# The partial sums of squares of eight RMS norms: added on VectorE, summed over partitions twice a norm

## The chip, the cores and the metric

One core of a Trainium2 chip runs the whole network of the reference in one launch. The metric is the device time of one execution in microseconds (us); what is compared are medians over several executions.

## The reference, cut to what matters

The input is one sequence of 256 tokens ("latents", 1024 features) with 256 context tokens beside it, all float32. The work is two blocks of two layers; a layer of the first block is a gated feed-forward network (ffn), a token mixer (mix) and a second ffn, a layer of the second is an attention mixer (even, odd) and a mixture of experts (peer). What matters here is that an RMS norm stands between every two of these parts:

```python
def rmsnorm(x, w):
    x32 = x.astype(jnp.float32)
    r = lax.rsqrt(jnp.mean(x32 * x32, axis=-1, keepdims=True) + EPS)
    return (x32 * r).astype(x.dtype) * w
...
    xl = xl + 0.5 * g1l * swiglu(modulate(rmsnorm(xl, norm_w[0]), sh1l, sc1l), w_ffn1_in, w_ffn1_out)
    ...
    hl = modulate(rmsnorm(xl, norm_w[1]), sh2l, sc2l)
    ...
    xl = xl + g2l * mix_l
    xl = xl + 0.5 * g3l * swiglu(modulate(rmsnorm(xl, norm_w[2]), sh3l, sc3l), w_ffn2_in, w_ffn2_out)
```

So for each token the squares of its 1024 features are summed, and the root's inverse scales the token.

## The kernel before

**Layout.** `x` and `h` are held as 128 partitions x KC = 8 chunks x tokens: feature 128 k + p of a token lies on partition p of chunk k. A stage works on T = 512 tokens (latents and context) or on TL = 256 (latents alone, where the context is no longer needed). A sum over a token's features is thus a sum over 8 chunks and then over 128 partitions.

**Split products.** Weights and activations are each split into a rounded high part and a low rest, and `split_product` (L1030 to L1034) makes three matmuls of them: high x high, high x low, low x high. ScalarE (ACT) rounds, VectorE (DVE) or GpSimd (POOL) subtracts to get the low part. A matmul has a 128x128 stationary operand (PEld loads it) and 512 or 256 moving columns.

**Stages.** They run one after the other, in this order: mods, norm1_0, ffn1_0, norm2_0, mix_0, norm3_0, ffn2_0, norm1_1, ffn1_1, norm2_1, mix_1, norm3_1, ffn2_1, final1, even_norm, even, peer_norm_0, peer_0, odd_norm, odd, peer_norm_1, peer_1, final2. Every engine has one queue of instructions, written in program order, and semaphores order the engines among each other. Weights come through a ring of 8 slots that SyncE (SP) fills; a slot is loaded again when `panel_done` (or, for modulation weights, `mod_units_read`) says that it has been read.

**The end of a stage, where the change lies.** An ffn ends with 8 output panels, one for each chunk dc of x. A panel is 22 chunks of the hidden layer x 3 matmuls = 66 matmuls (`ffn_stage` of the tensor block, L1129 to L1146); its weights come in two halves, each rounded by ACT (`round_out`, L1580) once the panel half that used the buffer before is through, and then split by DVE (`split_out`, L2054). The mixers (mix, even, odd) end with 8 panels of 8 x 3 = 24 matmuls (`out_product`, L1148 to L1177) with `round_proj` (L1637) and `split_proj` (L2114) for weights. There the first two panels are made up to their last input chunks before the last part of the attention is there, so panels 0 and 1 end close together. mix_0 and even have 2 buffers for rounded weights, so that panel 2's weights are rounded only once panel 0 is through; mix_1 and odd have 4.

After each panel `add_to_x` (L2043) adds it to chunk dc of x (`x_added`), `square` (L1527) on ACT squares the chunk into a scratch tile, and `sums` (L1088 to L1096) on TensorE multiplies the squares, as the stationary operand, by a column of ones: one output column for each 128 tokens, accumulated over the 8 chunks in one bank. One such product in float32 comes out as two pairs of weight load and matmul, so a chunk costs 8 pairs with 512 tokens and 4 with 256. The sums of chunk dc - 1 stand in TensorE's queue behind panel dc (`sums_behind`), so those of chunks 0 to 5 stand between panels, and those of 6 and 7 behind the last panel. After an ffn there is one scratch tile (the last chunk of `h`), after a mixer there are two (in `work`). Then `norm_stage` takes over: ACT rounds the next stage's first weight unit (L1515), then takes the root (L1549), DVE the reciprocal (L2017), TensorE spreads it over the partitions (L1078), and DVE scales x (L2022).

In three of the four ffns (ffn1_0, ffn2_0, ffn1_1) DVE also makes products for the modulation in between (`mod_sums`, L1948 and L1950): up to two weight units, 8 operations, in an output panel.

Norms that don't follow an ffn or mixer: norm1_0 (behind mods), even_norm (behind final1), odd_norm and final2 (behind peer).

## Time and profile before

| | |
|---|---|
| median of 3 runs | 4516.12 us (4515.93, 4516.12, 4524.71) |
| profiled execution | 4522.2 us, its span 4520.4 us |
| mean granted TensorE clock in it | 0.973 of full speed |
| TensorE busy | 4294.9 us, 95% of the span |
| VectorE busy | 3221.8 us, 71% |
| ScalarE busy | 1825.0 us, 40% |
| GpSimd busy | 1423.2 us, 31% |

The span is the time from the first to the last instruction of the profiled execution; 1.8 us of its own time lie around it. In the rows below a time is in us from the span's start, "x8" is a run of eight instructions shown as one row, and a bracket gives the idle time of the engine ahead of the row and what ended it.

### The profile page before, as it was taken

To read this page: it belongs to the slowest core of one execution; us is meant where nothing else is said; L and a number is where in the kernel's file an instruction comes from. 1 tells how busy PE (TensorE), PEld (TensorE's weight loads), DVE (VectorE), ACT (ScalarE), POOL (GpSimd) and SP (SyncE) were. 2 spreads that over 40 slices of the span, in tenths; PEclk is the share of its full clock that TensorE was granted. 3 is DMA by queue.
4 is the path that set the end of the run, shared out by engine and by line. 5 is a ranking of instruction groups with operands and counts; after the bars stand their busy time and mean duration, and the time that the engine had idled before them with its cause. 6 is when DMAs were issued, how large, how long until landed. Compare 5 with 4: busy or idle time off the path is not lost.

```text
span 4520.4 us, 62059 instructions
## 1 busy us (share of the span) xinstructions
PE 4294.9 (95%) x24455; PEld 3842.2 (85%) x24455; DVE 3221.8 (71%) x5137; ACT 1825.0 (40%) x2986; POOL 1423.2 (31%) x701
## 2 busy tenths in 40 slices
PE   7999899999999998999999899799999999999999
PEld 5887678887888798767899899799998799999887
DVE  5764547876887575464589899498886757785776
ACT  3233242233233434254233577233334544444444
POOL 0000300000000100000277688667772028665443
PEclk9999999999999998998999999899999999999999
DMA  6543214544544264201467799899995146678884
GB/s 269 221 158 124 75 38 177 223 177 184 226 184 183 93 246 169 79 34 47 133 218 236 244 331 330 289 373 351 359 352 181 39 166 220 211 243 275 288 288 163
DMA packets 286689, 926.50 MB, mean 205 GB/s; under 512 B 19136, under 2 KB 170816, under 8 KB 212288
## 3 DMA queue, kind: packets, MB, share of 16 engines
q1 hardware_dynamic: 249536, 788.30, 49.1%
q0 software_dynamic: 36864, 134.23, 8.4%
q8 instruction: 195, 3.19, 0.3%
q14 instruction: 94, 0.77, 0.1%
HBM read 837.52 MB, written 84.93 MB: 204 GB/s over the span
## 4 chain that ended last, share of the span: by engine, by line
PE 77%; DVE 12%; DMA 5%; ACT 3%; POOL 2%; issue 1%; SPq 0%; DVEq 0%; ACTq 0%; POOLq 0%
PE bank L1032 22%; PE bank L1034 21%; PE bank L1033 21%; DVE work L2356 3%; PE bank L1203 2%; PE bank L1397 2%; DMA gates<-work 2%; PE bank L1018 2%; PE bank L1187 2%; PE bank L1022 1%; PE bank L1094 1%; DMA work<-in_up_rows,work 1%; DVE work L2463 1%; POOL weight_ring_low L2611 1%; PE bank L1194 1%
## 5 line engine op out<-in xcount | busy, mean ns | idle before, releaser
L2611 POOL TENSOR_TENSOR weight_ring_low<-weight_ring,up_high 128x1024 fp32r<-128x1024 f32 x240 | 650.2, 2719 | 1138.4 <-ACT up_high L1761 1136.4
L1034 PE MATMUL bank<-peer_h_high,weight_ring_low 128*128 128x256 f32 (+2 forms) x2240 | 702.7, 314 | 0.0
L1032 PE MATMUL bank<-peer_h_high,up_high 128*128 128x384 f32 (+1 forms) x2048 | 648.5, 317 | 35.6 <-POOL weight_ring_low L2611 33.7
L1033 PE MATMUL bank<-h_low,up_high 128*128 128x384 f32 (+1 forms) x2048 | 638.2, 312 | 0.0
L1032 PE MATMUL bank<-h_high,in_high 128*128 128x512 f32 (+1 forms) x1280 | 465.3, 364 | 5.6 <-DVE weight_ring_low L2002 5.2
L1848 ACT ACTIVATE down_high<-weight_ring 128x1024 fp32r<-128x1024 f32 x256 | 257.4, 1054 | 517.0 <-PE bank L1034 511.5
L1034 PE MATMUL bank<-h_high,weight_ring_low 128*128 128x512 f32 (+1 forms) x1280 | 464.7, 363 | 0.0
L1033 PE MATMUL bank<-h_low,in_high 128*128 128x512 f32 (+1 forms) x1280 | 464.6, 363 | 0.0
L2578 POOL TENSOR_SCALAR h<-work,params 128x256 f32<-128x256 f32 x12 | 10.9, 921 | 1439.8 <-DVE work L2266 1439.8
L1034 PEld LDWEIGHTS bank<-peer_h_high,weight_ring_low 128*128 128x128 f32 x2240 | 429.8, 192 | 3.8
L1032 PEld LDWEIGHTS bank<-peer_h_high,up_high 128*128 128x128 f32 x2048 | 394.3, 193 | 40.6 <-POOL weight_ring_low L2611 38.3
L2620 POOL TENSOR_TENSOR weight_ring_low<-weight_ring,down_high 128x1024 fp32r<-128x1024 f32 x128 | 314.8, 2459 | 321.3 <-ACT down_high L1848 321.2
L2383 DVE TENSOR_TENSOR weight_ring_low<-weight_ring,down_high 128x1024 fp32r<-128x1024 f32 x128 | 307.1, 2399 | 150.1 <-ACT down_high L1848 150.1
L1033 PEld LDWEIGHTS bank<-h_low,up_high 128*128 128x128 f32 x2048 | 394.0, 192 | 0.0
L1032 PE MATMUL bank<-hidden_high,down_high 128*128 128x384 f32 x1016 | 339.5, 334 | 0.5 <-DVE hidden_low L2383 0.5
L1034 PE MATMUL bank<-hidden_high,weight_ring_low 128*128 128x384 f32 x1016 | 339.4, 334 | 0.0
L1033 PE MATMUL bank<-hidden_low,down_high 128*128 128x384 f32 x1016 | 339.4, 334 | 0.0
L1767 ACT ACTIVATE work<-bank 128x384 f32<-128x384 f32 (+1 forms) x256 | 112.3, 439 | 496.2 <-PE bank L1034 492.0
L1515 ACT ACTIVATE in_high<-weight_ring 128x2048 fp32r<-128x2048 f32 x88 | 168.7, 1917 | 330.3 <-PE bank L1034 310.8
L1032 PEld LDWEIGHTS bank<-h_high,in_high 128*128 128x128 f32 x1280 | 242.3, 189 | 45.2 <-issue 7.8
L1033 PEld LDWEIGHTS bank<-h_low,in_high 128*128 128x128 f32 x1280 | 242.3, 189 | 37.4
L1034 PEld LDWEIGHTS bank<-h_high,weight_ring_low 128*128 128x128 f32 x1280 | 242.2, 189 | 37.3
(364 smaller groups left out, 10527.3 us busy)
## 6 DMA issues: line engine op xcount, KB each, us to landing
weight_ring<-in_up SPq DMA_DIRECT2D x128, 1024.0 KB, 5.6
weight_ring<-in_down SPq DMA_DIRECT2D x128, 1024.0 KB, 6.6
weight_ring<-in_mod_w SPq DMA_DIRECT2D x112, 1024.0 KB, 5.4
weight_ring<-in_ffn_in SPq DMA_DIRECT2D x88, 1024.0 KB, 6.8
weight_ring<-in_ffn_out SPq DMA_DIRECT2D x64, 704.0 KB, 4.4
gates<-work SPq DMA_DIRECT2D x40, 1024.0 KB
gelu<-work SPq DMA_DIRECT2D x64, 384.0 KB
work<-gates SPq DMA_DIRECT2D x16, 1536.0 KB
```

The costliest lines, as they stand in the source:

```text
L1018: mm(ps[bank][:, 0:cols], w_high[:, k, w(j0 + kc)], high[:, kc, 0:cols], start=kc == 0, stop=False)
L1032: mm(dst, w_high, a_high, start=first, stop=False)
L1033: mm(dst, w_high, a_low, start=False, stop=False)
L1034: return mm(dst, w_low, a_high, start=False, stop=last)
L1187: mm(ps[m % 4][:, 0:j["nk"]], j["q"][q], j["k"], start=True, stop=True).then_inc(scores_done, 1)
L1515: A(high_of(name)[1][:, k % 2, :], ring[:, u % SLOTS, :], ACT.Copy).then_inc(in_rounded, 1)
L1767: A(gelu_out[:, n // 2 % 2, n % 2, 0:t], ps[UP_BANKS[n % 3]][:, 0:t], ACT.Gelu).then_inc(gelu_ready, 1)
L1848: A(down_high[:, m % 2, k, :], ring[:, u % SLOTS, k * D:k * D + D], ACT.Copy).then_inc(down_rounded, 1)
L2356: V.scalar_tensor_tensor(row, row, 1.0, picked_h, ALU.mult, ALU.mult, accum_out=picked_acts[:, q:q + 1])\
L2383: return V.tensor_tensor(dst, src, high.bitcast(F32), ALU.subtract)
L2611: G.tensor_tensor(ring_low[:, slot, w], ring[:, slot, w], up_high[:, n % 3, :].bitcast(F32), ALU.subtract)\
L2620: G.tensor_tensor(ring_low[:, slot, D:], ring[:, slot, D:], down_highs[l][:, m % 2, 1, :].bitcast(F32), ALU.subtract)\
```

## The change

For the eight norms that follow an ffn or a mixer (norm2_0, norm3_0, norm1_1, norm2_1, norm3_1, final1, peer_norm_0, peer_norm_1; `joined`), the squares of chunks 1 to 6 are no longer summed over partitions one by one. Chunk 0's squares lie in a tile that serves as the total; `join_squares` on DVE adds the squares of chunks 1 to 6 to it, each ahead of DVE's wait for panel k + 1. TensorE then sums over partitions twice: once the total of chunks 0 to 6, and once chunk 7, which ACT writes into the same tile after the first of the two is through. Both stand behind the last panel (`joined_sums`). Chunks 1 to 6 have two scratch tiles of their own: banks 4 and 5 of PSUM behind an ffn, two tiles of `work` behind a mixer. A square waits for the join that frees its tile. The other norms keep their way; the counts of `summed` are kept by stage.

```diff
@@ -424,7 +424,7 @@
         ones_ready, lam_sums, lam_exps = sem("ones_ready"), sem("lam_sums"), sem("lam_exps")
         params_loaded, x_loaded, ctx2_loaded = sem("params_loaded"), sem("x_loaded"), sem("ctx2_loaded")
         tables_loaded, gains_ready = sem("tables_loaded"), sem("gains_ready")
-        squares_made = sem("squares_made")
+        squares_made, squares_added = sem("squares_made"), sem("squares_added")
         slot_full = [sem(f"slot_full{s}") for s in range(SLOTS)]
         panel_done = sem("panel_done")
         passed = {e: sem(f"{e}_passed") for e in ("pe", "act", "dve", "pool")}
@@ -500,12 +500,12 @@
                 before = stages[i - 1][0]
                 s["order"] = (2, 3, 4, 5, 7, 6, 0, 1) if name == "odd_norm" else tuple(range(KC))
                 s["sum_bank"], s["scale_bank"] = (7, 4) if name == "final2" else (2, 5) if before == "peer" else (5, 4) if before == "final" else (7, 6)
-                s["before"] = before
+                s["before"], s["joined"] = before, before in ("ffn", "mix", "even", "odd")
                 if kind == "norm":
                     s["next"] = stages[i + 1][1:]
                 norm_of[stages[i - 1][1]] = name, s
         counts = dict(norm=0, added=0, ffn=0, free=4, square=0, root=0, lora=0, conv=0, tile=0, out=0, mod=0,
-                      peer=0, ptile=0, rtile=0, parts=0, scaled=0, normed=0, rounds=0, keys=0)
+                      peer=0, ptile=0, rtile=0, parts=0, scaled=0, normed=0, rounds=0, keys=0, summed=0, joined=0)
 
 
         take = scratch()
@@ -731,7 +731,11 @@
 
             if s["before"] in ("mods", "final"):
                 return h[:, k, :]
-            return h[:, KC - 1, :] if s["before"] == "ffn" else work[:, k % 2 * T:k % 2 * T + T]
+            if not s["joined"]:
+                return work[:, k % 2 * T:k % 2 * T + T]
+            if k in (0, KC - 1):
+                return h[:, KC - 1, :] if s["before"] == "ffn" else work[:, 0:T]
+            return ps[4 + k % 2][:, :] if s["before"] == "ffn" else work[:, (1 + k % 2) * T:(2 + k % 2) * T]
 
         def job(q, k, nk, v, scale, prep=None):
             return dict(q=q, k=k, nk=nk, v=v, scale=scale, prep=prep)
@@ -827,6 +831,8 @@
             if kind in ("norm", "final"):
                 counts["norm"] += 1
                 counts["square"] += KC
+                counts["summed"] += 2 if s["joined"] else KC
+                counts["joined"] += (KC - 2) * s["joined"]
                 counts["root"] += 1
                 counts["scaled"] += KC
             if kind == "norm":
@@ -1100,6 +1106,23 @@
                 if name in norm_of and 0 <= k < KC:
                     sums(*norm_of[name], k)
 
+            def joined_sums(name):
+
+
+                if name not in norm_of:
+                    return
+                name, s = norm_of[name]
+                q, t = at[name]["square"], s.get("t", TL)
+                for last in (False, True):
+                    if last:
+                        pe.wait_ge(squares_ready, q + KC)
+                    else:
+                        pe.wait_ge(squares_added, at[name]["joined"] + KC - 2)
+                    for tt in range(t // P):
+                        i = mm(ps[s["sum_bank"]][:, tt:tt + 1], squares_of(name, s, 0)[:, tt * P:tt * P + P], ones[:, 0:1],
+                               start=not last and tt == 0, stop=last, skip_group_check=True)
+                    i.then_inc(summed, 1)
+
             def norm_stage(name, s):
                 if s["before"] == "mods":
                     return
@@ -1142,8 +1165,7 @@
                             o = split_product(ps[dc % 4][:, 0:t], out_part(2 * dc + half)[:, w], ring_low[:, u % SLOTS, w],
                                               ffn_high(kc)[:, 0:t], ffn_low[:, kc, 0:t], kc == first_chunks[0], kc == second_chunks[-1])
                         o.then_inc(panel_done if half else out_half, 1)
-                    sums_behind(name, dc - 1)
-                sums_behind(name, KC - 1)
+                joined_sums(name)
 
             def out_product(name, t):
 
@@ -1172,9 +1194,7 @@
                     if dc >= OUT_BANKS:
                         pe.wait_ge(x_added, at[name]["added"] + dc - OUT_BANKS + 1)
                     product(dc, range(KC - late, KC) if dc < 2 else range(KC)).then_inc(panel_done, 1)
-                    if dc:
-                        sums_behind(name, dc - 1)
-                sums_behind(name, KC - 1)
+                joined_sums(name)
 
             def attention(name, beside_first_scores=lambda: None):
                 jobs, dsts, subs = job_lists[name]
@@ -1516,14 +1536,18 @@
 
             def square(name, s, k):
 
-                t, kc, buffers = s.get("t", TL), s["order"][k], 1 if s["before"] == "ffn" else 2
+                t, kc = s.get("t", TL), s["order"][k]
                 if s["before"] == "final":
                     act.wait_ge(scaled_ready, at[name]["scaled"] - KC + k + 1)
                     act.wait_ge(ctx2_loaded, 16)
                 else:
                     act.wait_ge(x_added, at[name]["added"] - KC + k + 1)
-                    if k >= buffers:
-                        act.wait_ge(summed, KC * at[name]["norm"] + k - buffers + 1)
+                    if not s["joined"] and k >= 2:
+                        act.wait_ge(summed, at[name]["summed"] + k - 1)
+                    if s["joined"] and k == KC - 1:
+                        act.wait_ge(summed, at[name]["summed"] + 1)
+                    elif s["joined"] and k >= 3:
+                        act.wait_ge(squares_added, at[name]["joined"] + k - 2)
                 A(squares_of(name, s, k)[:, 0:t], x[:, kc, 0:t], ACT.Square).then_inc(squares_ready, 1)
 
             def square_behind(name, k):
@@ -1545,7 +1569,7 @@
                 if "next" in s:
                     round_unit(*s["next"], 0)
                 if s["before"] != "mods":
-                    act.wait_ge(summed, KC * (at[name]["norm"] + 1))
+                    act.wait_ge(summed, at[name]["summed"] + (2 if s["joined"] else KC))
                     A(square_sum[:, tiles], ps[s["sum_bank"]][:, tiles], ACT.Sqrt, bias=eps[:, 0:1], scale=1.0 / D).then_inc(root_ready, 1)
                 if "next" in s:
                     round_unit(*s["next"], 1)
@@ -2044,6 +2068,16 @@
                                                ALU.mult, ALU.add)
                 return i
 
+            def join_squares(name, k):
+
+
+                if name in norm_of and 1 <= k < KC - 1:
+                    name, s = norm_of[name]
+                    t, total = s.get("t", TL), squares_of(name, s, 0)
+                    dve.wait_ge(squares_ready, at[name]["square"] + k + 1)
+                    wait_for(dve, squares_added, at[name]["joined"] + k - 1)
+                    V.tensor_tensor(total[:, 0:t], total[:, 0:t], squares_of(name, s, k)[:, 0:t], ALU.add).then_inc(squares_added, 1)
+
             def ffn_stage(name, s):
                 t, f0, p0 = s["t"], at[name]["ffn"] * FC, plan.panel0[name]
                 o0 = at[name]["ffn"] * KC
@@ -2088,6 +2122,7 @@
                 for dc in range(KC):
                     if dc + 1 < KC:
                         split_out(2 * dc + 2)
+                    join_squares(name, dc - 1)
                     dve.wait_ge(panel_done, p0 + 2 * FC + dc + 1)
                     add_to_x(dc % 4, s["gate"], dc, t).then_inc(x_added, 1)
                     if dc + 1 < KC:
@@ -2117,6 +2152,7 @@
             def add_outs(name, gate, t):
 
                 for dc in range(KC):
+                    join_squares(name, dc - 1)
                     dve.wait_ge(panel_done, proj_panel(name) + dc + 1)
                     add_to_x(dc % OUT_BANKS, gate, dc, t).then_inc(x_added, 1)
                     if dc + proj_buffers(name) < KC:
```

## Rows read from the trace of the kernel before

**Rows 1.** The profile page: span, busy time of TensorE, and the chain that ended last.
```profile
span 4520.4 us, 62059 instructions
...
PE 4294.9 (95%) x24455; PEld 3842.2 (85%) x24455; DVE 3221.8 (71%) x5137; ACT 1825.0 (40%) x2986; POOL 1423.2 (31%) x701
...
PE 77%; DVE 12%; DMA 5%; ACT 3%; POOL 2%; issue 1%; SPq 0%; DVEq 0%; ACTq 0%; POOLq 0%
```

**Rows 2.** Groups by line and shape, PE: the norms' sums (count, busy, mean; idle before).
```profile
L1094 PE MATMUL bank<-ones,work 128*128 128x1 f32 x288 | 41.3, 265 | 9.2 <-ACT work L1527 9.1
L1094 PE MATMUL bank<-ones,h 128*128 128x1 f32 x288 | 40.1, 262 | 4.6 <-ACT h L1527 4.6
```

**Rows 3.** Timeline of PE (start, duration), a seam of ffn1_0's output panels and the next sums.
```profile
312.23 0.39 PE L1034 MATMUL bank<-ffn_high_last,weight_ring_low 128*128 128x512 f32 x1
312.46 0.95 PE L1094 MATMUL bank<-ones,h 128*128 128x1 f32 x8
313.27 0.49 PE L1032 MATMUL bank<-ffn_high,out_high 128*128 128x512 f32 x1
...
328.37 0.94 PE L1094 MATMUL bank<-ones,h 128*128 128x1 f32 x8
```

**Rows 4.** Timeline of PE in ffn1_0's input panels, first and last of 55 rows.
```profile
199.68 0.39 PE L1034 MATMUL bank<-h_high,weight_ring_low 128*128 128x512 f32 x1
...
211.92 0.39 PE L1034 MATMUL bank<-h_high,weight_ring_low 128*128 128x512 f32 x1
```

**Rows 5.** Timeline of PE around mix_1's first two seams (256 columns).
```profile
1541.54 0.28 PE L1034 MATMUL bank<-parts_mix,weight_ring_low 128*128 128x256 f32 x1
1542.97 0.60 PE L1094 MATMUL bank<-ones,work 128*128 128x1 f32 x4 [1.16 <-ACT work L1527]
1543.44 0.36 PE L1032 MATMUL bank<-parts_mix,proj_more 128*128 128x256 f32 x1
...
1543.76 0.28 PE L1034 MATMUL bank<-parts_mix,weight_ring_low 128*128 128x256 f32 x1
...
1546.28 0.28 PE L1034 MATMUL bank<-parts_mix,weight_ring_low 128*128 128x256 f32 x1
...
1546.76 0.36 PE L1032 MATMUL bank<-parts_mix,proj_more 128*128 128x256 f32 x1
```

**Rows 6.** Timeline of PE and DVE around mix_0's first seam (512 columns).
```profile
620.28 0.39 PE L1034 MATMUL bank<-parts_mix,weight_ring_low 128*128 128x512 f32 x1
621.72 1.05 PE L1094 MATMUL bank<-ones,work 128*128 128x1 f32 x8 [1.05 <-ACT work L1527]
622.63 0.47 PE L1032 MATMUL bank<-parts_mix,proj_wide 128*128 128x512 f32 x1
...
621.17 1.23 DVE L2114 TENSOR_TENSOR weight_ring_low<-weight_ring,proj_wide 128x1024 fp32r<-128x1024 f32 x1 [0.27 <-ACT proj_wide L1637]
```

**Rows 7.** Groups by line and shape, DVE: an add-sized operation that reads a bank.
```profile
L2022 DVE TENSOR_TENSOR h<-x,bank 128x512 f32<-128x512 f32 x56 | 37.6, 682 | 13.2 <-PE bank L1078 13.2
...
L2022 DVE TENSOR_TENSOR h<-x,bank 128x256 f32<-128x256 f32 x16 | 6.5, 416 | 2.0 <-PE bank L1078 2.0
```

**Rows 8.** Timeline of DVE in ffn1_1's fullest output panel: last split, next residual add.
```profile
1377.26 1.62 DVE L2054 TENSOR_TENSOR weight_ring_low<-weight_ring,out_high 128x1408 fp32r<-128x1408 f32 x1
1381.00 0.88 DVE L2043 SCALAR_TENSOR_TENSOR x<-bank,gate,x 128x256 f32<-128x256 f32 x2 [2.11 <-PE bank L1034]
```

**Rows 9.** Timeline of DVE in ffn2_1's output panels, two residual adds one panel apart.
```profile
1738.32 0.48 DVE L2043 SCALAR_TENSOR_TENSOR x<-bank,gate,x 128x256 f32<-128x256 f32 x1 [0.86 <-PE bank L1034]
...
1746.68 0.48 DVE L2043 SCALAR_TENSOR_TENSOR x<-bank,gate,x 128x256 f32<-128x256 f32 x1 [0.86 <-PE bank L1034]
```

**Rows 10.** Timeline of PE, DVE and ACT at the end of mix_0.
```profile
660.16 0.95 PE L1094 MATMUL bank<-ones,work 128*128 128x1 f32 x8
...
660.36 0.88 DVE L2043 SCALAR_TENSOR_TENSOR x<-bank,gate,x 128x256 f32<-128x256 f32 x2 [5.52 <-PE bank L1034]
...
661.27 0.63 ACT L1527 ACTIVATE work<-x 128x512 f32<-128x512 f32 x1 [5.76 <-DVE x L2043]
662.30 1.91 ACT L1515 ACTIVATE in_high<-weight_ring 128x2048 fp32r<-128x2048 f32 x1 [0.39 <-issue]
```

**Rows 11.** A matmul of peer_1 after idle time, and busy time by stretch with PEclk.
```profile
3890.22 0.39 PE L1032 MATMUL bank<-peer_h_high,up_high 128*128 128x256 f32 x1 [1.94 <-DVE weight_ring_low L2383]
...
3891.00:3895.00 4.00, 4.00 (x23) 4.00 (x22) 3.96 (x3) 0.10 (x1) 1.41 (x1) 0.57 0.00 0
```

## The prediction

> **What bounds the kernel now.** I read the page first. TensorE is busy 4294.9 us of a span of 4520.4 us, and the chain that ended last runs through it for 77% [rows 1]. So an operation taken off TensorE is worth its time, if nothing else holds the same place. The page is only a mean, so I went to the groups by line for what the change touches: the norms' sums are 576 pairs of weight load and matmul, some 263 ns each if one believes the mean, 81 us busy together [rows 2]. That overstates them, since a matmul's duration holds its flight through the array and neighbours overlap. What counts is by how much a group of sums pushes the next matmul back, and that only the timeline tells.
>
> At a seam between two of ffn1_0's output panels, the last matmul of a panel starts at 312.23 and the first of the next at 313.27, 1.04 us later, with the 8 pairs of one chunk between them [rows 3]. Where no sums are, the 55 rows from 199.68 to 211.92 give 54 steps of 0.2267 us, and they go over a panel's end without a break [rows 4]. So 8 pairs push back by 1.04 - 0.23 = 0.81 us. The period tells a little more: 328.37 - 312.46 = 15.91 us from sums to sums, against 66 x 0.2267 = 14.96 us for the matmuls alone, so 0.95 us go with each seam; the 0.14 us beyond the gap are slow first steps of the next panel (its first matmul takes 0.49 where 0.39 is usual) [rows 3]. With 256 columns the plain step is (1546.28 - 1543.76) / 21 = 0.12 us (third to last of a panel's 24), the gap over 4 pairs 0.48, so 0.36 us of pushing back, and the two first steps take 0.32 where 0.24 is usual: 0.44 us a seam [rows 5]. In ffn2_1 the period says the same: 1746.68 - 1738.32 = 8.36 against 66 x 0.12 = 7.92 us [rows 9].
>
> **The change part by part.**
>
> *Sums taken off the seams.* In each of the eight norms the sums of chunks 0 to 5 go, those of chunks 6 and 7 are kept in number and place (as the total and chunk 7). Five norms work on 512 tokens, three on 256, so 6 x (5 x 8 + 3 x 4) = 312 pairs go. In the ffns all six seams are plain. ffn1_0, ffn2_0, ffn1_1: 3 x 6 x 0.95 = 17.1 us. ffn2_1: 6 x 0.44 = 2.6 us.
>
> *The first seam of a mixer* isn't plain: panels 0 and 1 end close together, and the sums of chunk 0 wait for its square. In mix_1 that is 1.16 us idle, and the whole seam takes 1543.44 - 1541.54 = 1.90 us [rows 5]. Panel 2 has its weights already (4 buffers), so the seam shrinks to one step: 1.78 us, with the slow steps 1.86. In mix_0 the seam takes 622.63 - 620.28 = 2.35 us, but what is late next is the split of panel 2's weights, which ends at 621.17 + 1.23 = 622.40 [rows 6]. So only 0.2 us are won there, since the 8 pairs lay in the shadow of that split. odd is built as mix_1 in this respect and even as mix_0. Five plain seams follow in each: mix_0 and even 2 x (0.2 + 5 x 0.95) = 9.9 us, mix_1 and odd 2 x (1.86 + 5 x 0.44) = 8.1 us.
>
> *The joins on DVE.* 48 adds come in. The nearest row is an operation of the same shape that reads a bank and `x`: 0.68 us with 512 columns, 0.42 with 256 [rows 7], so 30 x 0.68 + 18 x 0.42 = 28 us more on DVE. I cost them at nothing; this is the cover. In ffn1_1's panels with two modulation units, the fullest, DVE ends the split of the next panel's weights at 1378.88 and idles 2.11 us until the add at 1381.00 [rows 8]. DVE's work there hangs on the panel's start, so the shorter panel takes 0.95 of that and the join 0.68; 0.48 us stay, and the split itself, which TensorE needs, stands ahead of the join. In ffn2_1 the split hangs on the panel's half, so only the join is taken from 0.86 us [rows 9], and 0.44 stay. A mixer's panel holds add, split and join: 0.88 + 1.23 + 0.68 = 2.8 us of 24 x 0.2267 = 5.4, or 0.48 + 1.23 + 0.42 = 2.1 of 2.9. The square that a join waits for stands in ACT's queue behind the rounding for a later panel; in the ffns that is done half a panel before. In mix_1 the join of chunk 1 holds the add of panel 2 back by about 1.4 us (square and split of the early panels come late); behind it are the split for panel 6 and the add itself, and TensorE asks for that split only four panels later. If the cover were gone, each 0.1 us that all 48 joins pushed TensorE back would cost 4.8 us.
>
> *New waits.* A square of chunks 3 to 6 waits for a join, which is done about a panel before. SP's loads move with `panel_done`, nothing else of its queue changes, and POOL's queue isn't touched.
>
> *The end of a stage.* Chunk 7's square now waits also for the first of the two sums behind a mixer (behind an ffn it did already). In mix_0 those 8 pairs run from 660.16 to 661.11, the add it waits for anyway from 660.36 to 661.24, and the square starts at 661.27 [rows 10]. So the new wait ends 0.13 us before the old one: nothing, or at worst some 0.3 us for each of four mixers. The root stands behind a 1.91 us rounding as before [rows 10]. The first sums need the joins of chunks 1 to 6; in ffn1_1 I count the last one 2 us before the panel's end.
>
> *Sum.* 17.1 + 2.6 + 9.9 + 8.1 = 37.7 us. **Bounds**: if the slow first steps stay (they could belong to the seam and not to the sums), a seam is worth 0.81 or 0.36 us: 14.6 + 2.2 + 8.5 + 7.2 = 32.5 us. I take the higher one, because the plain rows go over panel ends without such steps [rows 4]. On the other side I see no more than 42 us, if late adds and half-speed steps elsewhere fall better.
>
> The Trainium skill ("TensorE: Matmul & The Clock Gate", section "LDWEIGHTS (loading the stationary operand)") prices a weight load by its columns alone, 128 / 1.2 = 107 ns, however few columns are multiplied. By it, as an estimate, the 296 pairs that don't lie in the shadow of a split would bring 31.6 us, and with the waits at the mixers' first seams 34.3 us; the seams of this trace give 0.95 / 8 = 0.119 us a pair with the slow steps and 0.101 without them, so it stands between my two sums.
>
> **The rivals.**
>
> *A, the slow steps stay:* 32.5 us less, that is 4484 us. For it: such steps also follow a seam where TensorE only waited. Against it: rows 4. 14%.
>
> *B, the ffn panels are held by the weights' chain and not by TensorE:* rounding, then split, each half a panel. Then the four ffns bring nothing: 9.9 + 8.1 = 18 us less, 4498 us. Against it: the idle time of DVE in rows 8 and 9 stands behind the split, not ahead of it. 6%.
>
> *C, the clock.* In peer_1 a matmul came 1.94 us idle, and in the stretch from 3891 to 3895 the granted clock was 0.57, mostly the lower level of 1.2 GHz [rows 11]: 23 matmuls where 4.00 / 0.12 = 33 fit. In mix_0's first seam the sums stood in the middle of such a gap; now TensorE idles from about 620.7 to 622.4 at a stretch. One fall cost 10 steps of 0.12 us there, 1.2 us; I put 1.5 us for one at mix_0, and even's gap is shorter. At most 3 us of the 37.7 for both. Part of the forecast's own spread; chance of a fall one in four. The Trainium skill (the same page, section "A second HAM failure mode: psum-queue depth-cycling") warns that short idle times between groups of matmuls make the clock swing; by that the removal could cost rather than gain at these two seams.
>
> *D, slower.* The joins stand in DVE's queue ahead of the adds. If the squares come late, the join holds add and splits, these hold the next panel, and that its square. It decides where a panel loses more than it wins: 0.48 us of cover and 0.95 won in ffn1_1, so a join would have to hold DVE 1.4 us beyond its own 0.68. At 1.5 us lost for each of the 48 joins the kernel would take 72 - 37.7 = 34 us more, 4550 us. Against it: the idle rows 8 and 9, and ACT's small share of 40% [rows 1]. 2%.
>
> *E, the change brings nothing*, because what is won before a norm is waited away behind it, on weights that come no sooner. DMA has 5% of the chain [rows 1], and the ring is loaded as slots come free, so its times move too. 3%, 4516 us.
>
> **How the numbers follow.** The forecast has 75%. The profiled execution took 4522.2 us (span 4520.4), 6 us above the median of 4516.1; a share of 37.7 / 4522.2 = 0.83% on the median is again 37.7 us, and less a quarter of a clock fall the time is 4479 us. Its own range is 4474 to 4483. A reaches to 4484, and runs of one kernel differ by some us (4515.93 to 4524.71), so the range is 4474 to 4488 us; B, D and E, 11%, are left out. This kernel can be told from no change at about 0.2%, 9 us: faster 0.95 (forecast, A, B), same 0.03 (E), slower 0.02 (D).
>
> **What would show it.** The group of the sums should have 264 pairs where 576 were. Between ffn output panels the step over a seam should be 0.23 us and the period 14.96 us (7.92 in ffn2_1); mix_1's first seam should close, mix_0's should end at the split. 48 new adds of 0.68 and 0.42 us stand on DVE ahead of the residual adds, with idle time still behind them. From the last panel to the root nothing should move. I am wrong if TensorE shows new idle time on L2054 or L2114 at the seams, if the first matmuls of a panel still take longer, if chunk 7's square waits for TensorE, or if the granted clock is lower in these stretches.

## The result, and the profile after

The changed kernel took 4480.14 us, the median of four runs (4474.47 to 4481.91), beside 4519.01 us for the kernel before: a ratio of 0.9915, with an interval from 0.9903 to 0.9928. (The kernel before has a fourth run here, of 4521.89 us, beside the three shown above.) The prediction was 4479 us, 0.9918 of the median shown, in a range of 4474 to 4488. The profiled execution took 4481.78 us, its span is 40.4 us shorter than that of before.

The page after, to be held against [rows 1]:

```profile
span 4480.0 us, 61516 instructions
...
PE 4258.5 (95%) x24143; PEld 3809.4 (85%) x24143; DVE 3228.8 (72%) x5185; ACT 1823.7 (41%) x2986; POOL 1429.5 (32%) x701
...
PE 78%; DVE 11%; DMA 5%; ACT 3%; POOL 2%; issue 1%; SPq 0%; DVEq 0%; ACTq 0%; POOLq 0%
```

TensorE has 24455 - 24143 = 312 instructions fewer and VectorE 48 more, as counted. TensorE's busy time fell by 36.4 us, its share of the chain didn't. The VectorE total went up by only 7.0 us, though the joins' own records come to 28 us. Records of neighbouring instructions overlap in part, and other groups moved too (the sum of all VectorE durations rose by 22.6 us), so a difference of busy totals doesn't price an edit.

The joins and the sums that are left, by line and form (count, duration as min/median/max, first and last start; then who waited for the line):

```profile
L2079 DVE TENSOR_TENSOR h<-h,bank x24: 414/682/689, 323.4 to 1747.5; 128x512 f32<-128x512 f32 x18, 128x256 f32<-128x256 f32 x6
L2079 DVE TENSOR_TENSOR work<-work x24: 419/555/693, 617.5 to 3600.7; 128x512 f32<-128x512 f32 x12, 128x256 f32<-128x256 f32 x12
```

```profile
L1122 PE MATMUL bank<-ones,h x56: 164/250/271, 402.5 to 1753.8; 128*128 128x1 f32 x56
...
L1122 PE MATMUL bank<-ones,work x48: 164/250/271, 648.6 to 3603.9; 128*128 128x1 f32 x48
```

With the 160 pairs of even_norm, odd_norm and final2, which the change leaves alone, these are 264, and the trace names no instruction that waited for a join.

A seam is the place in TensorE's queue between two output panels, and the period is the time from one such place to the next. TensorE's timeline in ffn1_0, over the seam that [rows 3] showed, and one panel on:

```profile
312.52 0.39 PE L1040 MATMUL bank<-ffn_high_last,weight_ring_low 128*128 128x512 f32 x1
312.75 0.39 PE L1038 MATMUL bank<-ffn_high,out_high 128*128 128x512 f32 x1
312.98 0.39 PE L1039 MATMUL bank<-ffn_low,out_high 128*128 128x512 f32 x1
...
327.48 0.39 PE L1040 MATMUL bank<-ffn_high_last,weight_ring_low 128*128 128x512 f32 x1
```

The step over the seam is 0.23 us where it was 1.04, the first matmuls of the panel take 0.39 like all others, and the period is 327.48 - 312.52 = 14.96 us where it was 15.91. So the slow steps went with the sums. In mix_1 the first seam [rows 5] is closed:

```profile
1518.25 0.28 PE L1040 MATMUL bank<-parts_mix,weight_ring_low 128*128 128x256 f32 x1
1518.37 0.28 PE L1038 MATMUL bank<-parts_mix,proj_wide 128*128 128x256 f32 x1
```

In mix_0 the first seam [rows 6] ends at the split. TensorE, and below it DVE:

```profile
613.58 0.39 PE L1040 MATMUL bank<-parts_mix,weight_ring_low 128*128 128x512 f32 x1
615.75 0.50 PE L1038 MATMUL bank<-parts_mix,proj_wide 128*128 128x512 f32 x1 [1.79 <-DVE weight_ring_low L2149]
...
614.47 1.23 DVE L2149 TENSOR_TENSOR weight_ring_low<-weight_ring,proj_wide 128x1024 fp32r<-128x1024 f32 x1 [0.27 <-ACT proj_wide L1661]
```

The split ends at 615.70 and the matmul starts at 615.75; the seam takes 2.17 us where it took 2.35, and after 1.79 us idle the steps are 0.35, 0.24 and then 0.23 us. The granted clock from 613 to 625 was 1.00, so it didn't fall.

What the change was worth, stage by stage. The stretch is that from the first matmul of a stage's output product to the start of its last one, in us, from TensorE's timeline. The second column is a second profile of the kernel before (experiment e5, below), which shows what a stretch does by itself. Further on, the mark of a norm is the start of the first matmul that spreads its scale over the partitions (L1078 before, L1084 after).

| stage | before | before again | after | after - before | predicted |
|---|---|---|---|---|---|
| ffn1_0 | 125.53 | 125.52 | 119.80 | -5.73 | -5.7 |
| mix_0 | 51.76 | 51.79 | 47.00 | -4.76 | -4.95 |
| ffn2_0 | 125.31 | 125.33 | 119.59 | -5.72 | -5.7 |
| ffn1_1 | 125.32 | 125.30 | 119.59 | -5.73 | -5.7 |
| mix_1 | 27.05 | 27.05 | 22.98 | -4.07 | -4.06 |
| ffn2_1 | 74.39 | 75.51 | 72.93 | -1.46 | -2.64 |
| even | 50.70 | 51.55 | 45.93 | -4.77 | -4.95 |
| odd | 27.05 | 27.04 | 22.99 | -4.06 | -4.06 |
| sum | | | | -36.3 | -37.7 |

One term is off, ffn2_1, and the second column says that this is less the change's doing than the stretch's. TensorE waits there once for the end of a queue of other work, before and after alike, and runs at the lower clock level behind it. TensorE's timeline of before (one line) and of after:

```profile
1720.24 0.51 PE L1032 MATMUL bank<-ffn_high,out_high 128*128 128x256 f32 x1 [4.81 <-DVE weight_ring_low L2054]
```

```profile
1694.01 0.58 PE L1038 MATMUL bank<-ffn_high,out_high 128*128 128x256 f32 x1 [4.82 <-DVE weight_ring_low L2088]
1694.38 0.42 PE L1039 MATMUL bank<-ffn_low,out_high 128*128 128x256 f32 x1
1694.60 0.42 PE L1040 MATMUL bank<-ffn_high,weight_ring_low 128*128 128x256 f32 x1
```

and busy time by stretch (window, length, busy us and count of PE, PEld, DVE, ACT, POOL, then the granted clock, the DMA share and GB/s), of after and then of before:

```profile
1695.00:1700.00 5.00, 5.00 (x26) 5.00 (x25) 0.88 (x1) 0.00 (x0) 0.00 (x0) 0.50 0.00 0
1700.00:1710.00 10.00, 10.00 (x85) 10.00 (x85) 3.73 (x3) 4.11 (x4) 0.00 (x0) 0.99 0.39 144
```

```profile
1719.00:1723.00 4.00, 2.75 (x13) 2.76 (x14) 3.12 (x3) 1.22 (x2) 0.00 (x0) 0.67 0.38 153
1723.00:1728.00 5.00, 5.00 (x41) 5.00 (x41) 0.52 (x1) 1.38 (x1) 0.00 (x0) 0.92 0.00 0
```

Granted 0.50 is the lower level of 1.2 GHz; a step takes 0.21 us there and 0.12 at 2.4 GHz. By the trace's clock records the lower level lasted from 1693.3 to 1700.2 after the change, 6.8 us, and from 1720.4 to 1723.8 before it, 3.4 us, behind idle times of 4.82 and 4.81 us. So 28 steps were slow and not 16, and 12 x 0.09 = 1.1 us of the 1.2 that are missing are these. In the second profile of before the lower level also lasted 6.8 us. Like is thus compared with like in 75.51 - 72.93 = 2.58 us (6.8 us both), and in the 2.83 us that e1 won against the first profile (3.4 us both), beside 2.64 predicted. even scatters too, with its mixer's sums at the seams: 50.70 and 51.55 us before, 51.95 in e1.

### The profile page after: what moved, and what is told of

Same layout as the page of the kernel before. It is cut to its first block, busy times and chain, and to the rows that moved or that the text cites. A ratio compares the mean times of both kernels' runs of the same rounds, so it can differ in the third digit from the quotient of the medians.

```text
span 4480.0 us, 61516 instructions
## 1 busy us (share of the span) xinstructions
PE 4258.5 (95%) x24143; PEld 3809.4 (85%) x24143; DVE 3228.8 (72%) x5185; ACT 1823.7 (41%) x2986; POOL 1429.5 (32%) x701
## 4 chain that ended last, share of the span: by engine, by line
PE 78%; DVE 11%; DMA 5%; ACT 3%; POOL 2%; issue 1%; SPq 0%; DVEq 0%; ACTq 0%; POOLq 0%
PE bank L1038 22%; PE bank L1040 22%; PE bank L1039 22%; DMA gates<-work 2%; DVE work L2392 2%; PE bank L1223 2%; PE bank L1417 2%; PE bank L1024 2%; PE bank L1207 2%; PE bank L1028 1%; DMA work<-in_up_rows,work 1%; POOL weight_ring_low L2647 1%; PE bank L1214 1%; DVE weight_ring_low L2026 1%; DVE work L2499 1%
## 5 line engine op out<-in xcount | busy, mean ns | idle before, releaser
L1038 PEld LDWEIGHTS bank<-peer_h_high,up_high 128*128 128x128 f32 x2048 | 394.5, 193 | 39.4 <-POOL weight_ring_low L2647 37.1
L1974 DVE SCALAR_TENSOR_TENSOR weight_ring<-weight_ring,params 128x1024 f32<-128x1024 f32 x224 | 273.9, 1223 | 0.0
L1972 DVE SCALAR_TENSOR_TENSOR params<-weight_ring,params 128x1024 f32<-128x1024 f32 x224 | 273.7, 1222 | 0.0
```

Of the source, the lines that this page charges most:

```text
L1038: mm(dst, w_high, a_high, start=first, stop=False)
L1972: V.scalar_tensor_tensor(mod_product, w, 1.0, cond_rows[:, 0, :], ALU.mult, ALU.mult, accum_out=mods[:, chunk + c, 0:1]).then_inc(products ...
L1974: i = V.scalar_tensor_tensor(w, w, 1.0, cond_rows[:, 1, :], ALU.mult, ALU.mult, accum_out=mods[:, chunk + c, 1:2])
```

## The experiments

Ratios are to runs of the kernel before that were taken on the same chip beside them, with the 95% interval. The twelve kernels:

| kernel | median us | ratio | interval | span us |
|---|---|---|---|---|
| e1, joins behind the ffns alone | 4494.94 | 0.9946 | 0.9933 to 0.9959 | 4496.1 |
| e2, joins behind the mixers alone | 4498.95 | 0.9954 | 0.9941 to 0.9966 | 4502.8 |
| e3, the change, idle pairs at the seams | 4506.33 | 0.9976 | 0.9967 to 0.9985 | 4499.8 |
| e4, the change, more work ahead of each join | 4484.16 | 0.9923 | 0.9909 to 0.9936 | 4484.1 |
| e5, the kernel before | 4519.35 | 1.0002 | 0.9993 to 1.0011 | 4514.0 |
| e6, the change, ffn2_1's gains later | 4473.66 | 0.9909 | 0.9894 to 0.9924 | 4466.4 |
| e7, the change, even_norm joined too | 4475.71 | 0.9912 | 0.9898 to 0.9925 | 4473.0 |
| e8, e6 and e7 together | 4475.78 | 0.9906 | 0.9891 to 0.9922 | 4482.3 |
| e9, the changed kernel | 4477.62 | 0.9915 | 0.9901 to 0.9928 | 4478.9 |
| e10, as e3 | 4505.84 | 0.9977 | 0.9968 to 0.9986 | 4504.5 |
| e11, as e6 | 4474.27 | 0.9912 | 0.9897 to 0.9927 | 4474.1 |
| e12, as e8 | 4470.53 | 0.9903 | 0.9888 to 0.9918 | 4466.8 |

**e1 and e2: each half of the change alone.** The norms left out keep their sums between the panels.

```diff
-s["joined"] = before in ("ffn", "mix", "even", "odd")
+s["joined"] = before in ("ffn",)                  # e1
+s["joined"] = before in ("mix", "even", "odd")    # e2
...
+                    at_seam(name, dc)             # behind each panel: sums_behind(name, dc - 1) where not joined
```

> Only the four norms behind an ffn are joined, the four behind a mixer keep their sums at the seams. If the gain is TensorE's time at the seams, it is additive: 17.2 us in the three ffns with 512 columns and 1.5 to 2.6 us in ffn2_1, so 19 to 20 us below before (ratio 0.9957), and the output panels of the mixers take what they took before (51.8, 27.1, 50.7, 27.1 us). If the ffn panels were held by the weights' chain (rival B), this kernel would stand within 0.1% of before.

> Only the four norms behind a mixer are joined. By my theory 4.8 us in each of mix_0 and even (five seams of 0.95 and 0.2 at the first) and 4.1 us in each of mix_1 and odd (five of 0.44 and 1.9 at the first, where TensorE no longer waits for a square): 17.7 us below before (ratio 0.9961). If rival B held, all of the change's gain would be here, 38 us.

Measured: 22 us less for the ffns, 18 us less for the mixers, by the medians beside 4517.08 for the kernel before. The output stretches say where. In e1 those of the ffns fell by 5.71, 5.72, 5.72 and 2.83 us against the first profile of before, and mix_0, mix_1 and odd stayed within 0.3, but even, which e1 leaves alone, took 1.26 us more; in e2 the mixers' fell by 5.01, 4.06, 4.05 and 4.06, and ffn1_0, ffn2_0 and ffn1_1 stayed within 0.01. The two losses of ratio add up to 0.54% + 0.46% = 1.00%, the whole change has 0.85% with 0.72 to 0.97 as its interval, and each half is known to 0.13% either way, so the medians don't tell the two sums apart; the eight stretches of both halves, 20.0 + 17.2 = 37.2 us, make what the whole has, 36.3, and neither half hides behind the other. In e1 the ffn2_1 stretch gained 2.83 us, against 2.64 predicted, and in e2, where nothing of it was changed, it was 1.22 us longer: the clock behind its wait again.

**e3: the seams' pairs put back, with nothing to do.** The joins stay. After each of panels 1 to 6 TensorE gets as many one-column products as the sums had, of constants, into unused columns of the bank. They wait for nothing and nobody reads them.

```diff
+            def at_seam(name, dc):
+                s = norm_of[name][1]
+                if 1 <= dc <= KC - 2:
+                    for tt in range(s.get("t", TL) // P):
+                        mm(ps[s["sum_bank"]][:, 8 + tt:9 + tt], ident, ones[:, 0:1], start=tt == 0, stop=True, skip_group_check=True)
```

> The changed kernel, all joins in place, but at each of the 48 seams TensorE runs as many pairs of weight load and matmul as before (8 or 4), on a constant tile and into unused columns, so that they wait for nothing. By my theory all comes back but the waits for a square at the first seams of mix_1 and odd (2 x 1.16 us): 2 us below before (ratio 0.9995), and the ffn period is 15.9 us again. A rival says that the gain comes from ACT and the scratch tiles, since squares no longer wait for sums: then the time stays at that of the changed kernel, 38 us below before.

TensorE's timeline in ffn1_0:

```profile
312.49 0.40 PE L1040 MATMUL bank<-ffn_high_last,weight_ring_low 128*128 128x512 f32 x1
312.72 0.95 PE L1114 MATMUL bank<-ones,params 128*128 128x1 f32 x8
313.53 0.48 PE L1038 MATMUL bank<-ffn_high,out_high 128*128 128x512 f32 x1
...
328.59 0.95 PE L1114 MATMUL bank<-ones,params 128*128 128x1 f32 x8
```

The gap is 313.53 - 312.49 = 1.04 us and the period 15.87, as before the change with 1.04 and 15.91; the first matmul takes 0.48 us again. So the seam's cost and the slow step come with the pairs, whatever they multiply, and not with the squares, the waits or the bank. All eight output stretches together are within 4.7 us of before, and 3.0 of these are the 1.51 and 1.50 us of mix_1 and odd, whose first seams no longer wait 1.16 us for a square. This repeats in e10 (-1.51 and -1.51; the ffns' -0.24 to -0.28). So the rival in e3's expectation, that the gain comes from squares that no longer wait for sums, holds for 4.7 us at most, these 3.0 among them.

But the kernel is 0.24% below before, not the 0.05% that I expected, which its interval excludes, so it was measured again.

> The kernel with idle pairs at the seams once more. Its output panels gave 4.7 us over before, its median 10.8. If the rest was spread of peer_0 (1350.9 us in its profile, 1354 to 1358 in others), the ratio is now nearer to 0.999; if joined kernels are faster elsewhere too, it is again 0.9976.

It came out as 0.9977, the same.

So 5 to 6 us of the idle-pair kernel's 10 to 11 lie outside of the stretches that the pairs touch, in stages whose work is the same. The largest piece is even, from its norm's mark to its first output product: 265.34 and 264.00 us in the two profiles of before, 261.18 and 261.21 here. There 1.5 us are the clock. The stretches of 5 us that begin with the same matmul (0.77 us in before, behind 2.43 us idle), of before, then of e3:

```profile
1894.88:1899.88 5.00, 5.00 (x16) 4.05 (x17) 1.94 (x1) 0.00 (x0) 0.00 (x0) 0.70 0.33 138
```

```profile
1888.44:1893.44 5.00, 5.00 (x22) 4.14 (x23) 1.94 (x1) 0.00 (x0) 0.00 (x0) 1.00 0.35 147
```

After the same wait the lower level came in the one and not in the other. The same holds for the kernel as a whole: by the clock records its two profiles spent 225 and 224 us at the lower level, and those of before 249 and 238. The other runs agree. The mean granted clock of the 11 runs of e3 is 0.9745 and of e10 0.9748, and that of the runs of before beside them 0.9735 and 0.9733. As an estimate, if TensorE had work all the while, 0.0010 and 0.0015 of some 4505 us are 4.5 and 6.8 us, about the 5 to 6 that are missing. So the rest fits the clock; why the kernel with idle pairs met less of the lower level isn't settled, and this doubt of some us stands beside every sum of this case.

**e4: how much cover the joins have.** Ahead of each join VectorE reduces a piece of a constant tile, 1856 columns with 512 tokens and 928 with 256, into an unused cell.

```diff
+                    dve.wait_ge(tables_loaded, 16)
+                    steps.wait()
+                    steps.count(V.tensor_reduce(small[:, 14:15], params[:, lay["cos1"][0]:lay["cos1"][0] + 1856 * t // T], AX, ALU.max))
                     V.tensor_tensor(total[:, 0:t], total[:, 0:t], squares_of(name, s, k)[:, 0:t], ALU.add).then_inc(squares_added, 1)
```

> The changed kernel with one further DVE operation of about 2.0 us (1.0 us with 256 columns) ahead of each join, a maximum over a constant tile whose result nobody reads: it measures the cover. By my count DVE then has about 15.8 us of work in an ffn1_1 panel with two modulation units, against a period of 14.96, and about 1 us of reserve; it holds TensorE only in runs of such panels: 1.5 to 3 us above the changed kernel, 35 to 37 us below before (ratio 0.992). If DVE's queue set the pace at the seams (rival D), 48 operations of 1 to 2 us would cost 50 us or more and the kernel would be slower than before.

The reduces took 2.08 and 1.11 us, three times a join's own time. The output stretches are those of the changed kernel to 0.1 us (-5.73, -4.68, -5.72, -5.71, -4.06, -1.48, -4.76, -4.07): no seam noticed 30 x 2.08 + 18 x 1.11 = 82 us more on VectorE. The 4 us that it lost (4484.1 against 4480.0) are at four stage ends, which took 1.37 us more behind ffn2_0, 1.48 behind ffn1_1, 0.64 and 0.66 behind mix_1 and odd. VectorE and then TensorE at the end of ffn1_1:

```profile
1391.55 2.09 DVE L2081 TENSOR_REDUCE small<-params 128x1 f32<-128x1856 f32 x1
1393.55 0.69 DVE L2082 TENSOR_TENSOR h<-h,bank 128x512 f32<-128x512 f32 x1
```

```profile
1392.62 0.39 PE L1040 MATMUL bank<-ffn_high_last,weight_ring_low 128*128 128x512 f32 x1
1394.29 1.05 PE L1122 MATMUL bank<-ones,h 128*128 128x1 f32 x8 [1.29 <-DVE h L2082]
```

The last join now ends after the last panel, and the first sums wait 1.29 us for it. So the cover ends first at the last join of a stage, not at the seams where I had counted it: I had expected the loss at the fullest panels, from the 0.48 us left there, but the split that TensorE needs stands ahead of the join, and what is late behind it has time.

**e5 and e9: the kernel before and the changed kernel as entries of their own.**

> The kernel before itself, once more, for a second profile and a null comparison. Its output panels should take what they took (125.5, 51.8, 125.3, 125.3, 27.1, 74.4, 50.7, 27.1 us, within 0.3 but for clock falls in ffn2_1); what differs elsewhere is the spread of executions. If the stretches outside of the output panels are as fast here as in the third experiment (a span of 4500 us), the 6 us that the third had beyond its seams are spread; if the median ratio is 1.000 and no profile of before is that fast, something in the joined kernels is faster outside of the seams, and my sum misses it.

> The changed kernel once more, beside the three others of this set on one chip. The output panels should repeat within 0.3 us (119.8, 47.0, 119.6, 119.6, 23.0, 72.9, 45.9, 23.0 us, but for clock falls in ffn2_1 and even). The two middles that could hide a cost of the change, norm3_0's and norm1_1's first input panels, should again stand 1.4 us above the first profile of before; if they do in every joined kernel and in no profile of before, it is the change's. Ratio 0.9915 within 0.001.

The ratios are 1.0002 and 0.9915, so before agrees with itself, and the change is worth what it was the first time. The second profile of before is 6.4 us shorter than the first (4514.0), 3.6 of them in peer_0 (from peer_norm_0's mark to odd_norm's), a stage of one expert product after the other that took between 1350.9 and 1371.8 us in the profiles of this case, whatever was changed. The second profile of the changed kernel has the stretches of the first to 0.15 us (ffn2_1 72.91, even_norm's stage 16.70).

Both expectations set a test, and each finds something outside of the seams that goes with the edits. No profile of before is as fast as e3's span of 4500 us; the clock figures above belong to that. For the two middles (from a norm's mark to the first output product), norm1_1's is spread: 246.36 and 247.96 us in the two profiles of before, 247.83 after. norm3_0's isn't: 246.29 and 246.33 us before, 247.69 and 247.66 after, and 247.0 to 247.8 in all twelve profiles of kernels with joins. The granted clock in the first 12 us behind its mark, of before, then of after:

```profile
664.62:676.62 12.00, 9.33 (x36) 7.52 (x37) 10.78 (x13) 11.41 (x19) 0.00 (x0) 0.72 0.00 1
652.75:664.75 12.00, 9.34 (x30) 7.53 (x31) 9.88 (x12) 10.54 (x18) 0.00 (x0) 0.59 0.01 5
```

So up to 1.4 us there go with the joins, as a cost. A third middle goes the other way: norm3_1's took 138.86 and 139.04 us before and 139.00 in e1, where the mixers keep their sums, but 137.0 to 137.1 in all nine profiles with joined mixers and no idle pairs (137.8 with idle pairs). A window around the same 2.57 us of idle time, of before, then of after:

```profile
1583.00:1595.00 12.00, 9.43 (x67) 9.26 (x66) 5.25 (x4) 4.41 (x5) 0.00 (x0) 0.86 0.47 177
1558.24:1570.24 12.00, 9.43 (x79) 9.26 (x78) 6.03 (x5) 5.08 (x5) 0.00 (x0) 1.00 0.56 212
```

That clock fall is absent with joined mixers, which is worth 1.8 us. Both effects repeat with the edit; by which step a closed seam moves a clock fall further on isn't shown.

**e6: the work that ffn2_1's first seam waits for, moved behind it.** ACT makes an Exp with a table load and loads the root's table ahead of rounding panel 1's weights, DVE makes biases and gains ahead of splitting them. Both go one or two weight units later.

```diff
-                if name == "ffn2_1":
-
-                    act.wait_ge(lam_sums, 1)
-                    A(lam_tmp[:, 2:4], lam_tmp[:, 0:2], ACT.Exp).then_inc(lam_exps, 1)
-                load_roots(name)
+                if name != "ffn2_1":
+                    load_roots(name)
                 for v in range(2, 2 * KC):
                     round_out(v)
+                    if name == "ffn2_1" and v == 3:
+                        act.wait_ge(lam_sums, 1)
+                        A(lam_tmp[:, 2:4], lam_tmp[:, 0:2], ACT.Exp).then_inc(lam_exps, 1)
+                        load_roots(name)
...
-                if name == "ffn2_1":
-                    add_biases(len(plan.mod_read), trunk, MODS)
-                    second_gains()
                 for dc in range(KC):
                     if dc + 1 < KC:
                         split_out(2 * dc + 2)
+                    if name == "ffn2_1" and dc == 0:
+                        add_biases(len(plan.mod_read), trunk, MODS)
+                        second_gains()
```

> The changed kernel; in ffn2_1 alone the Exp and the loads of two tables on ACT stand behind the rounding of weight halves 2 and 3, and DVE's biases and gains behind the split of half 2. TensorE's idle 4.8 us ahead of panel 1 should shrink to about 0.5: 4.5 us, and if the clock does not fall then, up to 3 us more, since from 1694 to 1700 it ran at the lower level: 4.5 to 7.5 us below the changed kernel, 43 to 46 below before (ratio 0.990). Rival: the chain of Exp and table loads only moves and holds half 4, then 0 to 2 us.

> The changed kernel with the later Exp, table loads and gains in ffn2_1. Its panels there took 65.8 us where the changed kernel took 72.9, so 7 us below the changed kernel: ratio 0.990. If the clock's lower stretch only moves, 0.9910 or more.

Of e6, TensorE's timeline at that seam, and busy time and granted clock behind it:

```profile
1688.72 0.39 PE L1038 MATMUL bank<-ffn_high,out_high 128*128 128x256 f32 x1 [0.34 <-DVE weight_ring_low L2089]
```

```profile
1692.00:1700.00 8.00, 8.00 (x69) 8.00 (x69) 3.70 (x3) 4.12 (x6) 0.00 (x0) 1.00 0.44 152
```

The wait went from 4.82 to 0.34 us, and the clock stayed at its upper level. ffn2_1's stretch took 65.76 us in e6 and 65.77 in e11, 7.2 less than after the change: 4.5 of waiting, and 28 steps (6 us / 0.214) at 0.21 instead of 0.12, 2.6 us. The ratios, 0.9909 and 0.9912, don't stand clear of 0.9915 by their intervals, and e11's median is only 3.4 us below e9's, where 7 were expected; what is shown is the stretch, twice. Part is given back behind it: from even_norm's mark to even's first output product the granted clock was 0.95 in e6 and e11 and 0.97 in e9, and that stretch took 1.0 us longer (265.26 and 265.33 us against 264.31). From norm3_1's mark to peer_norm_0's the two took 6.7 and 6.6 us less than e9.

**e7: even_norm joined too.** It stands behind final1 and was left as it was: 64 pairs on TensorE with nothing beside them. VectorE adds its eight squares, TensorE sums once.

```diff
+                if s.get("whole"):
+                    for k in range(1, KC):
+                        dve.wait_ge(squares_ready, at[name]["square"] + k + 1)
+                        wait_for(dve, squares_added, at[name]["joined"] + k - 1)
+                        V.tensor_tensor(h[:, 0, :], h[:, 0, :], h[:, k, :], ALU.add).then_inc(squares_added, 1)
...
```

> The changed kernel with even_norm joined as well: its squares lie in eight tiles of h, DVE adds chunks 1 to 7 to chunk 0 and TensorE sums once, 8 pairs where 64 stand now and where nothing covers them (14 us from the first pair to the last). The scaling of final1 ends at 1758.9, seven joins of 0.61 after one another take 4.3, eight pairs at the lower clock 1.7: the root at about 1765.3 where it was at 1770.7, so 5 us below the changed kernel, 43 below before (ratio 0.9904). Rival: DVE's queue is the longer one here, scaling and joins one behind the other, and TensorE wakes cold: 2 us or less.

TensorE's timeline from even_norm's start, of the changed kernel and of e7:

```profile
1754.58 1.07 PE L1084 MATMUL bank<-params,small 128*128 128x128 f32 x4 [0.55 <-DVE small L2041]
1756.89 13.81 PE L1100 MATMUL bank<-ones,h 128*128 128x1 f32 x64 [1.24 <-ACT h L1551]
1771.27 2.07 PE L1084 MATMUL bank<-params,small 128*128 128x128 f32 x8 [0.57 <-DVE small L2041]
```

```profile
1752.15 1.07 PE L1084 MATMUL bank<-params,small 128*128 128x128 f32 x4 [0.55 <-DVE small L2049]
1762.22 1.87 PE L1132 MATMUL bank<-ones,h 128*128 128x1 f32 x8 [8.99 <-DVE h L2046]
1764.65 2.08 PE L1084 MATMUL bank<-params,small 128*128 128x128 f32 x8 [0.56 <-DVE small L2049]
```

From mark to mark the stage took 1764.65 - 1752.15 = 12.50 us where it took 16.69: 4.2 less. The pairs took 13.81 / 64 = 0.216 us each, at the lower level, against 0.119 at a seam; now TensorE waits 8.99 us for the additions instead. The 5 us expected for the kernel aren't shown: here too the stretch behind took 0.9 us longer (265.26), and the ratio of 0.9912 doesn't stand clear of 0.9915.

**e8 and e12: both.**

> The two before this one together. They lie in different stretches, so they add: 9 to 12 us below the changed kernel, 48 to 50 below before (ratio 0.989). A rival, that gains so close to each other (15 us apart) share one clock fall, gives 7 to 8 us.

> Later gains and joined even_norm together. By the stretches in its profile it gives 7.2 and 4.5 us over the changed kernel, 11 to 12 in all: ratio 0.989. In its first runs it gave 0.9906 and its profile spent 1371.8 us in peer_0, 14 us more than others. If that was one execution's spread, the ratio falls to 0.989 and peer_0 is back at 1351 to 1358; if peer_0 is slow again, the earlier start costs it something, and what is gained ahead of it is given back there.

The first gave 0.9906 with a span of 4482.3, more than that of the changed kernel. Its stretches were right (ffn2_1 65.77, even_norm's stage 12.22), but its profile has peer_0 at 1371.8 us, 15.5 more than after. In e12 peer_0 is back at 1353.7 and the span is 4466.8, with ffn2_1 at 65.77 and even_norm's stage at 12.19. Its median of 4470.53 is 45.5 us below the kernel before and 7 below e9; the two stretches have 11.7, less 0.7 and 0.8 us in even, whose stretch took 46.69 and 46.76 in the two profiles and 45.99 in e9. The ratio of 0.989 that was expected both times didn't come (0.9906 and 0.9903), and only the second interval holds it. It is the fastest measured version, but beside 0.9915 its lead isn't certain.

## Why the prediction was right

- **The plain seams** were costed at 0.95 us with 512 columns. The three long ffns gave 5.73, 5.72 and 5.73 us for six seams, 0.955 each, the sum's 17.1 us almost to the digit. This term was read off the period between two seams and not off the sums' own durations, which would have said 8 x 0.26 = 2.1 us a seam.
- **The slow first steps** were the open choice between 37.7 and 32.5 us, rival A. They are gone with the sums in the changed kernel and back with idle pairs in e3, so A is refuted. With 0.81 us a seam ffn1_0 would have won 4.9 us.
- **The first seams of the mixers.** mix_1 and odd won 4.07 and 4.06 for 4.06 predicted. Of this 1.5 us each came from the join by itself, since e3 has it with the pairs still there. mix_0 and even won 4.76 and 4.77 for 4.95: the first seam 0.18 for 0.2, the five others 0.92 and not 0.95. The 1.78 us behind one step, and the shadow of the split, were as read [rows 5, 6].
- **ffn2_1** is the term that came out off: 1.46 for 2.6 between these two profiles. Where the lower clock level lasted equally long on both sides it is 2.58 and 2.83 (e1), so the price of the seams was right. They closed (the panel's period is 1712.51 - 1704.59 = 7.92 us, as costed); what moved is the length of the lower clock behind a wait that the change doesn't touch.
- **The joins at nothing.** Right, with more room than I gave them: the seams took four times the joins' work without a sign (e4). Rival D, that joins hold back the next panel, is refuted for delays of up to 2.1 us a join. In ffn2_1 DVE idles 0.53 us behind a join, where I had 0.44.
- **Rival B**, that the weights' chain holds the ffn panels, is refuted by the 14.96 us period: it is 66 plain steps. **Rival E**, that the gain is waited away behind the norm, is refuted: the norms' marks of after stand ahead of those of before by 5.5, 11.9, 16.3, 20.5, 24.5 and 27.7 us from norm2_0 to final1, by 26.5 at even_norm and 40.4 at the end. Of what the stretches won, 1.4 us were given back behind norm3_0's mark and 1.2 in even_norm's stage, and neither was a wait for weights: TensorE's waits behind norm3_0 add up to 5.2 us before and 4.9 after, those in even_norm's stage to 2.3 in both.
- **Rival C**, a clock fall at mix_0's first seam, didn't come, though TensorE now idles there for 1.79 us at a stretch instead of 1.05. Nor did it come at that seam in any other profile with joined mixers, and the clock didn't swing between the groups of matmuls there. The quarter of a fall in the forecast (0.4 us) was thus not needed. The clock falls that did move lie elsewhere, behind norm3_0 and norm3_1, where the forecast had no term.
- **The end of a stage** didn't move by more than 0.3 us (last matmul to the scale's mark: -0.09 behind the ffns, -0.27 behind mix_0), as costed. What came unlooked for is that the 8 pairs that spread the scale ran at the lower level in some profiles (2.08 us against 1.33, in norm2_0), up to 0.9 us per norm.
- **What lies outside.** 40.4 - 36.3 = 4.1 us of the spans' difference are in no output stretch. Two pieces of it repeat, and the prediction had both at nothing: norm3_1's middle is 1.8 us shorter wherever the mixers are joined, and norm3_0's is up to 1.4 longer wherever anything is. The others are single profiles' differences: peer_1's stage has 2.4 us, peer_0's 1.8 (1358.07 to 1356.29), mix_0's middle 1.3 and even's 1.0; norm1_1's middle took 1.5 back and even_norm's stage 1.2.
- **How much of it is luck.** The mechanism and the price of a seam were right by the timeline, to 0.1 us in five of the eight stretches and to 0.2 in two more. That 4479 and 4480.14 us lie 1.1 us apart is luck: the four runs of the changed kernel alone differ by 7.4 us, 38.9 us is the medians' difference where 37.1 were forecast, and the pieces outside of the stretches happened to add up to little.

The Trainium skill ("TensorE: Matmul & The Clock Gate", section "LDWEIGHTS (loading the stationary operand)") prices a weight load by its columns alone, 107 ns for 128, which came out as an estimate of 34.3 us in the prediction. The trace comes near: the stretches have 36.3 us here and 37.2 in the two halves, and a plain seam 0.119 us a pair, 0.101 of it without the slow steps behind the group (0.14 us a group).

## What to carry to other kernels

A short group of small products in a stream of large ones costs what it pushes the stream back, with the first steps behind it; read that off the period between two such groups, against a stretch without them, and then off the one seam where something else ends last. If a stage is bound by TensorE and VectorE idles in it, the summing over chunks can be done by adds there, and the first place where that would hurt is the last add before the consumer, not the fullest panel. A wait of some us in such a stream costs a second time by the clock behind it: taking away 4.5 us of waiting brought 7.2 in its own stretch, of which 6.6 were left some stages on.

## What the runs showed of the hardware that I had not expected

- Behind the same idle time of 4.8 us at the same place the lower clock level lasted 3.4 us in one profile of the kernel before and 6.8 us in the other. Behind the same 2.43 us idle in even it came in one (0.70 over 5 us) and not in the other (1.00). A difference of 1 to 1.5 us in one stretch between two single profiles thus need not be an effect of the edit.
- A difference that repeats in every profile with an edit can still be the clock's: here an edit in one stage went with a clock fall in the next stage that stayed away (norm3_1, 1.8 us) or lasted longer (norm3_0, 1.4 us).
- A matmul of 512 columns behind a group of one-column pairs takes 0.48 us where 0.39 is usual, also if the pairs depend on nothing (e3). Behind mere idle time it does too: 0.50 us behind 1.79 us idle at mix_0's first seam, at a granted clock of 1.00. So the slow first steps go with the break in the stream, and need no pair in it.
- The same expert stage, with instructions that no kernel here changes, took 1350.9 to 1371.8 us for it; a span can thus be off by ten us or more while every stretch that an edit touches repeats to 0.1 us.
- The kernel with idle pairs is 0.24 and 0.23% faster than before in two measurements, of which its output stretches explain less than half. The mean granted clock of its runs is higher by 0.0010 and 0.0015; why it is isn't settled.
